# Row length of four matmul operands 528 to 576 floats, and the last stage's operands begun at column 0

## The reference

```python
h = concat([meta, x])                                   # 528 x 1024
for layer in (0, 1):
    h = h + 0.5 * swiglu(rmsnorm(h), w_gate, w_up, w_down)        # 1024 -> 2816 -> 1024
    hn = rmsnorm(h)
    mix = conv_ssm_mixer(hn) if layer == 0 else window_attention(hn)
    if layer == 1: h = h[16:]; mix = real rows only     # the meta rows are dropped here
    h = h + mix
    h = h + 0.5 * swiglu(rmsnorm(h), ...)
```

## Time and profile before

| | |
|---|---|
| median of three runs | 1912.97 us |
| profiled execution: span from first to last instruction | 1910.1 us |
| TensorE matmul busy | 1895.6 us, 13887 matmuls |
| VectorE busy | 956.5 us |
| ScalarE busy | 599.5 us |
| GpSimd busy | 351.3 us |
| granted TensorE clock, mean over the span | 0.999 of full |

### The profile page before, as it was taken

One profiled execution on the slowest core, in us unless ns is written; L12 is line 12 of the kernel. 1 busy time (PEld: TensorE's weight loads), 2 busy tenths in 40 slices (PEclk: granted clock), 3 DMA queues, 4 the chain that ended last, 5 costly groups with the idle time before them and its releaser, 6 DMA issues.

```text
span 1910.1 us, 33827 instructions
## 1 busy us (share of the span) xinstructions
PE 1895.6 (99%) x13887; PEld 1788.7 (94%) x13887; DVE 956.5 (50%) x1077; ACT 599.5 (31%) x707; POOL 351.3 (18%) x629
## 2 busy tenths in 40 slices
PE   8999999999999999999999999999999999999999
PEld 8999999999999999999999999999987778888887
DVE  5443356668765443344554433345557654434443
ACT  5222222332243222222342222223456532222232
POOL 2888789314230000000000000000012000000000
PEclk9999999999999999999999999999999999999999
DMA  6322444547523332432243323322321233233322
GB/s 180 89 83 83 140 145 126 160 127 189 125 67 89 89 86 83 117 86 74 69 124 88 83 83 99 89 80 69 111 72 45 67 89 100 81 98 100 104 69 86
DMA packets 330785, 188.29 MB, mean 99 GB/s; under 512 B 8152, under 2 KB 323832, under 8 KB 330712
## 3 DMA queue, kind: packets, MB, share of 16 engines
q1 hardware_dynamic: 323296, 166.81, 31.5%
q0 software_dynamic: 7088, 20.38, 4.1%
q10 hardware_dynamic: 328, 0.07, 0.0%
HBM read 174.91 MB, written 11.14 MB: 97 GB/s over the span
## 4 chain that ended last, share of the span: by engine, by line
PE 96%; DVE 2%; issue 1%; ACT 1%; ACTq 0%; POOL 0%; DVEq 0%
PE ps L793 79%; PE ps L1009 5%; PE ps L1051 2%; PE ps L1120 2%; PE ps L1070 1%; PE ps L1259 1%; PE ps L1221 1%; PE ps L1161 0%; PE ps L970 0%; PE ps L969 0%; PE ps L960 0%; PE ps L838 0%; PE ps L1182 0%; PE ps L853 0%; PE ps L1172 0%
## 5 line engine op out<-in xcount | busy, mean ns | idle before, releaser
L793 PE MATMUL ps<-xl,wh 128*128 128x264 f32 (+1 forms) x2432 | 564.5, 302 | 0.0
L793 PE MATMUL ps<-xh,wh 128*128 128x264 f32 (+1 forms) x2432 | 563.5, 301 | 0.8 <-DVE t_a L1610 0.7
L793 PE MATMUL ps<-xh,wl 128*128 128x264 f32 (+1 forms) x2432 | 563.2, 301 | 0.0
L1557 DVE TENSOR_TENSOR wl<-raw,wh 128x2048 fp32r<-128x2048 f32 x171 | 399.9, 2339 | 172.8 <-ACT wh L1270 172.8
L1270 ACT ACTIVATE wh<-raw 128x2048 fp32r<-128x2048 f32 x172 | 327.7, 1905 | 253.0 <-PE ps L793 211.2
L793 PEld LDWEIGHTS ps<-xh,wh 128*128 128x128 f32 x2432 | 390.4, 188 | 17.7 <-DVE t_a L1610 0.9
L793 PEld LDWEIGHTS ps<-xl,wh 128*128 128x128 f32 x2432 | 389.3, 189 | 15.5 <-issue 0.2
L793 PEld LDWEIGHTS ps<-xh,wl 128*128 128x128 f32 x2432 | 389.0, 189 | 14.8
L793 PE MATMUL ps<-act_h,wh 128*128 128x264 f32 (+1 forms) x1232 | 285.1, 301 | 0.0
L793 PE MATMUL ps<-act_l,wh 128*128 128x264 f32 (+1 forms) x1232 | 285.1, 301 | 0.0
L793 PE MATMUL ps<-act_h,wl 128*128 128x264 f32 (+1 forms) x1232 | 284.7, 301 | 0.0
(11 more groups left out here) (308 smaller groups left out, 1721.0 us busy)
## 6 DMA issues: line engine op xcount, KB each, us to landing
raw<-in_ff_w_gate SPq DMA_DIRECT2D x88, 512.0 KB, 4.0
raw<-in_ff_w_up SPq DMA_DIRECT2D x87, 512.0 KB, 5.2
raw<-in_ff_w_down SPq DMA_DIRECT2D x64, 384.0 KB, 4.1
raw<-in_ff_w_down SPq DMA_DIRECT2D x64, 320.0 KB, 3.7
raw<-in_even_w_in SPq DMA_DIRECT2D x16, 512.0 KB, 5.4
raw<-in_attn_w_qkv SPq DMA_DIRECT2D x12, 512.0 KB, 4.3
raw<-in_even_w_out SPq DMA_DIRECT2D x8, 512.0 KB, 4.6
raw<-in_attn_w_o SPq DMA_DIRECT2D x8, 512.0 KB, 4.7
```

The lines of the kernel that those rows point to most:

```text
L793: last = nc.tensor.matmul(ps[:, 2 * pair + hf, 0:nh], w[:, slot, b * P:(b + 1) * P], x[:, k0 + k, c0 + hf * nh:c0 + (hf + 1) * nh], start= ...
L1557: v.tensor_tensor(wl[:, c % 2, :], raw[:, c % 2, :], wh[:, c % 2, :].bitcast(F32), ALU.subtract).then_inc(wl_ready, 1)
```

## The change

Rows of `xh`, `xl`, `act_h` and `act_l` become 576 floats long (2,304 bytes, nine times 256), of which 528 are used. For the feed-forward 3 and the output projection the operands are written and read from column 0 (`FRONT`) in place of column 16; `h`, the PSUM tiles and the temporaries keep their columns. The query and key/value projections keep column 16. To make room, the scratch for DMA descriptors shrinks from 16,384 to 8,192 bytes in each partition.

```diff
+    ROW = -(-L // 64) * 64
+    FRONT = (0, SEQ, 1)
-        xh = sb("xh", [P, KD, L], F32R)
-        xl = sb("xl", [P, KD, L], F32R)
-        act_h = sb("act_h", [P, PART[0], L], F32R)
-        act_l = sb("act_l", [P, PART[0], L], F32R)
+        xh = sb("xh", [P, KD, ROW], F32R)[:, :, 0:L]
+        xl = sb("xl", [P, KD, ROW], F32R)[:, :, 0:L]
+        act_h = sb("act_h", [P, PART[0], ROW], F32R)[:, :, 0:L]
+        act_l = sb("act_l", [P, PART[0], ROW], F32R)[:, :, 0:L]
+        def operand(col):
+            return FRONT if col == REAL else col
...
-                mm3(pair, slot, blocks, xh, xl, 0, col, before).then_inc(tile_full, 1)
+                mm3(pair, slot, blocks, xh, xl, 0, operand(col), before).then_inc(tile_full, 1)
...
-                            mm3(s, (u0 + s) % 2, range(nf), act_h, act_l, 0, col,
+                            mm3(s, (u0 + s) % 2, range(nf), act_h, act_l, 0, operand(col),
...
             def out_part(d, k0, k1, sums=None):
-                c0, width, _ = REAL
+                c0, width, _ = FRONT
...
-                nc.scalar.activation(xh[:, d, cols], h[:, d, cols], ACT.Copy,
+                nc.scalar.activation(xh[:, d, span(operand(col))], h[:, d, cols], ACT.Copy,
...
-    nc = _bacc.Bacc("TRN2", target_bir_lowering=False, num_devices=1)
+    nc = _bacc.Bacc("TRN2", target_bir_lowering=False, num_devices=1, dynamic_dma_scratch_size=8192)
```

More of the change, by code:

```diff
@@ L1309, in gate_up @@
                             act.wait_ge(gated[n], k + 1)
-                            nc.scalar.activation(act_h[:, s + 2 * i, cols], t_c[:, cols], ACT.Copy).then_inc(act_h_done[n], 1)
+                            nc.scalar.activation(act_h[:, s + 2 * i, span(operand(col))], t_c[:, cols], ACT.Copy).then_inc(act_h_done[n], 1)
                     gate_up(0, part == 0)
@@ L1502, in out_high @@
                 act.wait_ge(o_full, n + 1)
-                nc.scalar.activation(act_h[:, 2 * g:2 * g + 2, META + j * P:META + (j + 1) * P].rearrange("p t (c n) -> p t c n", c=2),
+                nc.scalar.activation(act_h[:, 2 * g:2 * g + 2, j * P:(j + 1) * P].rearrange("p t (c n) -> p t c n", c=2),
                                      ps[:, 0:2, 0:P].rearrange("p c (t n) -> p t c n", t=2), ACT.Copy).then_inc(oh_done, 1)
@@ L1577, in scaled_low @@
                 gain = vec[:, GAIN[m] + d:GAIN[m] + d + 1] if isinstance(d, int) else vec[:, bass.ds(d + GAIN[m], 1)]
-                v.scalar_tensor_tensor(xl[:, d, cols], h[:, d, cols], gain, xh[:, d, cols].bitcast(F32), ALU.mult, ALU.subtract).then_inc(x_ready, 1)
+                v.scalar_tensor_tensor(xl[:, d, span(operand(col))], h[:, d, cols], gain, xh[:, d, span(operand(col))].bitcast(F32), ALU.mult, ALU.subtract).then_inc(x_ready, 1)
             def rms(m, col):
@@ L1617, in gate_up @@
                             dve.wait_ge(act_h_done[n], k + 1)
-                            v.tensor_tensor(act_l[:, s + 2 * i, cols], t_c[:, cols], act_h[:, s + 2 * i, cols].bitcast(F32), ALU.subtract).then_inc(act_ready[n], 1)
+                            v.tensor_tensor(act_l[:, s + 2 * i, span(operand(col))], t_c[:, cols], act_h[:, s + 2 * i, span(operand(col))].bitcast(F32), ALU.subtract).then_inc(act_ready[n], 1)
                         if first and n == 0:
@@ L1983, in out_low @@
                 dve.wait_ge(oh_done, n + 1)
-                cols = lambda x: x[:, 2 * g:2 * g + 2, META + j * P:META + (j + 1) * P].rearrange("p t (c n) -> p t c n", c=2)
+                cols = lambda x: x[:, 2 * g:2 * g + 2, j * P:(j + 1) * P].rearrange("p t (c n) -> p t c n", c=2)
                 v.tensor_tensor(cols(act_l), ps[:, 0:2, 0:P].rearrange("p c (t n) -> p t c n", t=2),
```

## The result

The changed kernel takes 1881.95 us, the median of five runs (1879.44 to 1882.17), against 1912.39 us (1911.57 to 1914.33) for five runs of the kernel before. The ratio is 0.9837 with a 95% interval of 0.9825 to 0.9848: 30.4 us or 1.6% less, where the forecast was 14.7 us less and the range ended at 1886. The sign and the place were right, the size was half of what came.

A forecast was written before the change was run, and what follows sets the result against it. The prediction took TensorE's matmul-to-matmul time as the bound. Its terms, 11.8 + 3.3 - 0.3 - 0.1 = 14.7 us less, took the median from 1912.97 to 1898.3 us, with a range of 1886 to 1912 us.

The forecast's parts named there:

- What bounds the kernel: Whole kernel: TensorE's matmuls cover 1895.6 of 1910.1 us, so time changes only through how fast one matmul follows another.
- The address has a say, and equal residues are the cheapest: Matmul rows: those starting at 128 are cheapest; moving and stationary operand at the same residue (modulo 256 bytes) fits all.
- The hint from the key and value projection: Weights moving at 128: rows take 0.69 to 0.70 us, 693 ns with activations at 128 too; bounds the 512-column gain at 1.3 us.
- the price of a row after the change: All changed rows cost what rows at 128 cost before: 727.5 ns for 264 columns, 689.7 ns for 512.
- the rival on the slow side: All rows settle in the dear phase, 739.7 and 699.5 ns: 1925.9 us; chance of slower 0.10.
- 264 columns: 1,792 rows of six matmuls, 734.1 to 727.5 ns: 11.8 us less, bounds 2.0 and 22.6 us.
- 512 columns: Feed-forward 3 and output projection, 592 rows, 695.2 to 689.7 ns: 3.3 us less.
- Query: Query projection keeps column 16, its 64 rows all at residue 192, the dear one: 0.3 us more.
- Key and value: Key and value projection, 32 rows with activations at 192, 698 ns against 695: 0.1 us more.
- Register instructions and scratch: Nine VectorE register instructions before `xl` writes in second down parts, and halved descriptor scratch for GpSimd's transfers: nothing counted.
- That nothing changes: Rival: the residue only chooses where in an eight-row pattern time falls; 1912.97 us, or 1910.1 with bad values; chance 0.15.
- the excess goes away altogether: Rival: unequal starts cause all excess, rows fall to 660 and 640 ns: 165 us less, 1748 us; chance 0.03.

The follow-up runs named there:

- the small kernel: Separate kernel streaming only matmuls of one kind per section, none of the trunk computed: 512 columns at equal residues 226.7 ns, at distance 64 228.9 ns.
- The small kernels: Matmul-only kernels with uniform distances, rows in turn, or narrower weights: 512 columns at 0 and 64 in turn 232.8 ns, at four distances in turn 231.7 ns.
- the two runs above: Changed kernel with column 16 kept for feed-forward 3 and output projection, 1885.49 us; changed kernel with moving tensors 64 bytes further, weights unmoved, 1906.42 us.
- the changed kernel's second profile: The changed kernel run again unaltered, beside the run with query, key and value projections also from column 0: 1881.47 us, ratio 0.9838.

## Why the forecast was half the size

**What bounds the kernel** was right. TensorE's start-to-start time is nearly the whole kernel, and 30.1 us of span came with the same 13,887 matmuls.

**The address has a say, and equal residues are the cheapest** was right for 512 columns, and was shown: 228.9 ns at distance 64 whichever of the two operands is shifted, 226.7 ns at four different equal residues, and 1906 us with 64 bytes between them. For 264 columns it was right in part and by luck in part. The prediction took 128 for the one cheap start because k = 0 was the cheapest kind of row; alone, the start of k = 3 (distance 192/224) costs 120.0 ns as well, and its 734.0 ns of before were those of a row among others. The hint from the key and value projection was weaker than it seemed: its undisturbed rows of before take about 698, 693, 696 and 693 ns for k = 0, 1, 2, 3 modulo 4, so activations at residue 0 (k = 1) came out as cheap as those at 128 (k = 3). Equal residues were a guess that fitted, and the small kernel proved it.

**The step that failed is the price of a row after the change.** The prediction read the price of a row at 128 among the rows of before, "the middle of the two values that a row at 128 has today, 727.5 ns", and 689.7 ns for 512 columns, and used it for a stream in which all rows are so. The trace of before had no such stream. The runs show that the cost is not a row's own: 0 and 64 in turn take 232.8 ns where each alone takes 226.7 and 228.9, and with rows of 544 floats half the rows are at distance 0 and none of them gets its 680 or 720 ns (the lowest are 696 and 721). In place of 727.5 it is 720.0, in place of 689.7 it is 680.0. The text had written that "what ran before has a say as well", and used it for the rival on the slow side, and for the low bound it allowed only the best value that any row had (721.5). It did not allow a value below every row of before, which is what a stream without changes gives at distance 0.

The small kernels also divide the gain. At their own prices the four kinds of rows of before would have averaged 728 ns (720, 732, 740 and 720) and 690.9 ns (three times 230.3). By an estimate from that, 7.5 ns x 1,792 + 10.3 ns x 592 = 20 us of the gain is the better distance, and 6.1 ns x 1,792 + 4.3 ns x 592 = 13 us is that the rows no longer differ. The forecast left the second out: it priced the new rows by one that still paid for its neighbours.

The terms, each as measured from the chain's pieces and the rows:

- 264 columns: 11.8 us forecast. The pieces give 734.1 - 720.5 = 13.6 ns a row, x 1,792 = 24.4 us. The bound of 22.6 was too narrow.
- 512 columns: 3.3 us forecast. 695.2 - 680.6 = 14.6 ns, x 592 = 8.6 us.
- Query, 0.3 us more forecast: wrong in sign. The rows fell from 697.2 to 688.1 ns, because alike rows at distance 64 cost less than mixed ones (686.7 ns in the two runs above); 64 x 9.1 = 0.6 us less. Key and value, 0.1 us more forecast: they rose from 694.5 to 699.8 ns, 32 x 5.3 = 0.2 us. They are alone at distance 192 now, and 699.8 is close to three times that distance's 233.4.
- Register instructions and scratch, nothing forecast: nothing found. The scratch was tried alone. The register instructions were not, and no wait in the trace names them.

These terms make 33.4 us, and the span fell by 30.1. About 3 us of the difference are seen. The first is the granted clock at the start. The first 60 us of the changed kernel and, below it, of the kernel before:

```profile
0.00:60.00 60.00, 53.28 (x390) 52.10 (x391) 31.57 (x44) 28.95 (x40) 21.19 (x48) 0.94 0.62 161
...
0.00:60.00 60.00, 52.45 (x393) 51.25 (x394) 31.89 (x44) 28.93 (x40) 21.78 (x48) 0.97 0.62 161
```

The clock (third number from the end) is lower because it stands at 0.50, the 1.2 GHz level, for 6.8 us after a pause of TensorE, where it did so for 3.4 us before. After the first hundred matmuls the changed kernel is 0.9 us behind. Both lengths occur with either layout, so this is put down to the execution and not to the change: the changed kernel's second profile and that of the kernel before with the small scratch have 6.8 us, the changed kernel with column 16, with the shift of 64 bytes and with all starts at 0 has 3.4. The second is the mixer's input projection, whose rows are broken up by other work and went from 731.6 to 720.9 ns only: 128 x 2.9 = 0.4 us. The third is pauses: distances of 0.29 us and more between starts add up to 35.1 instead of 33.2 us.

One of these pauses is a wait that the prediction had not seen. At 350.56 us a load of weights takes 10.94 us and stands in the chain (the median of its kind is 3.7 to 4.0 us), and TensorE pauses for 1.5 us at 364.6. Before, the pause of this stretch came earlier in the order, at 336.5 us, with 0.95 us. The load begins while GpSimd moves its finished tables about. With TensorE ahead of its old times the load no longer has cover; that the tables' transfers slow it is the reading that fits, and was not tried.

**The rivals.** That nothing changes is refuted, and with it what the prediction made of the 16-byte lines that the Trainium skill gives for SBUF (Advanced Engine Details and Errata, SBUF Cachelines). The Trainium skill doesn't compare start addresses there; that all starts on such a line are as good was inferred, and 512 columns at 0, 64 or 128 bytes from the weights take 226.7, 228.9 and 232.4 ns. That the excess goes away altogether is refuted too: 13.4 ns remain over 213.3. The rival on the slow side did not come with rows of 576 floats: like rows settled in the cheap state. That a row's cost hangs on the row before it is real, and with rows of 544, which differ in turn, it made the kernel slower than before: 1922.69 us.

**What stays open** is why distance and rhythm matter. At distance 0 the excess does not fall with the width of the weights: a load of 32 fp32r columns takes 108 ns, near the 98 ns of the bf16 load, and the matmuls still take 231.7 ns where bf16 takes 215.8. That points to the 4-byte moving stream at the full clock, but no run had one operand of 4 bytes and the other of 2, so it is argued and not shown. (Where the granted clock was 0.50, from 14.3 to 21.1 us in the changed kernel, 264 columns take 220 ns, which is 264 columns at 1.2 GHz with no excess at all.) How this stream meets the 128-column load of weights, and why two halves 1,024 bytes apart cost 3.3 ns more than one start, is not settled.

## What to carry to other kernels

When TensorE is the bound, read the distance from start to start, and by place in the job: a pattern over k that repeats with the row length in memory is a layout cost. For fp32r matmuls of 512 columns, give the moving operand rows of a multiple of 256 bytes and start it at the same residue as the weights, so that the distance never changes; padding to another length can cost more than none. For another width, time the stream first: of these placements 264 columns have several that are as cheap, 256 columns do better at distance 64, and two halves both at the weights' residue are worse than the second 32 bytes on. And don't price a uniform stream by its rows in a mixed one: a short kernel that runs the stream alone gave it to about 0.1 ns here (120.0 and 226.7 against 120.1 and 226.7 in the chain).

## What the runs showed of the hardware that was not expected

- fp32r matmuls of 512 columns with 128 weight columns take from 226.7 ns (start residues equal, modulo 256 bytes) to 236.7 ns (4 bytes off). bf16 takes 215.8 ns at both distances tried, 0 and 64. The bf16 values, 215.8 and 112.5 ns, are those that the Trainium skill gives for an isolated gap (TensorE: Matmul & The Clock Gate, Back-to-back issue gap); the fp32r ones are 11 and 7.5 ns above it.
- The cost has memory: streams at distance 0 and 64 take 226.7 and 228.9 ns, the two in turn 232.8 ns by threes and 230.8 ns one by one. Distances 128 and 192 take 232.5 and 233.4 ns alone and 231.0 ns in turn.
- fp32r matmuls of 264 columns in pairs take 120.0 ns at distances 0/32, 160/192, 192/224 and 224/0, and 123.3 ns at 128/160 and with two halves both at 0. The extra at distance 128 goes with the weight load: 123.4, 121.0 and 120.0 ns with 128, 64 and 32 weight columns.
- fp32r matmuls of 128 and of 192 columns take the same 111.7 ns, and 256 take as long as 264, 120 ns (all at distance 0). At distance 64, 256 columns take 117.8 ns.
